# Experts of the mixture stage: which ones share a pass, and in which order the passes run

## The reference

```python
def _hier_moe(h, rg_w, rg_b, re_w, re_b, w_gate, w_up, w_down):
    pg = jax.nn.softmax((ht @ rg_w + rg_b).astype(f32), axis=-1)
    g_val, g_idx = lax.top_k(pg, 1)                      # one of 4 groups
    le = (jnp.einsum('td,ode->toe', ht, re_w) + re_b).astype(f32)
    le = jnp.take_along_axis(le, g_idx[:, :, None], axis=1)[:, 0]
    pe = jax.nn.softmax(le, axis=-1)
    e_val, e_idx = lax.top_k(pe, TOPK_EXPERT)            # 2 of its 8 experts
    ...
    for o in range(N_GROUPS):
        hid = jax.nn.silu(einsum(ht, w_gate[o])) * einsum(ht, w_up[o])
        out = out + jnp.einsum('tef,efd->td', hid * c_o[:, :, None], w_down[o])
```

| group | experts | tokens |
|---|---|---|
| 0 | 0 to 7 | 72 101 67 73 27 38 39 99 |
| 1 | 8 to 15 | 83 98 70 46 47 50 69 97 |
| 2 | 16 to 23 | 110 55 30 40 37 52 94 44 |
| 3 | 24 to 31 | 94 59 51 48 72 42 89 55 |

## Time and profile before

### The profile page before, as it was taken

How to read it: one execution, slowest core, us unless ns; L and a number is a source line. 1 busy time by engine, 2 the same in 40 slices (tenths; PEclk the granted TensorE clock), 3 DMA queues, 4 the chain that set the end, 5 groups by cost and what they waited for, 6 DMA issues and landing times. The chain is left out here.

```text
span 1122.4 us, 13494 instructions
## 1 busy us (share of the span) xinstructions
PE 1015.0 (90%) x5111; PEld 597.1 (53%) x5111; DVE 495.0 (44%) x1214; ACT 274.6 (24%) x629; POOL 161.3 (14%) x150
## 2 busy tenths in 40 slices
PE   6999999975599989999999999996999999979980
PEld 4434777764455456666667455563554444434430
DVE  3477560068815466665665124274721211212214
ACT  3200110130112377566655011120101110101113
POOL 3000000025301131201010000011212122111210
PEclk9999999986899999999999999987999999989995
DMA  9200020032400091000000243455889999999728
GB/s 257 90 19 25 1 76 0 1 43 75 96 1 1 1 256 52 2 1 2 1 2 2 75 150 125 193 218 226 270 305 361 378 390 390 378 367 363 271 49 306
DMA packets 53632, 163.16 MB, mean 145 GB/s; under 512 B 24759, under 2 KB 26871, under 8 KB 41207
## 3 DMA queue, kind: packets, MB, share of 16 engines
q1 hardware_dynamic: 45184, 144.38, 35.8%
q0 software_dynamic: 8384, 17.91, 6.5%
HBM read 145.28 MB, written 26.29 MB: 153 GB/s over the span
## 5 line engine op out<-in xcount | busy, mean ns | idle before, releaser
L1885 PE MATMUL banks<-shared,wout 128*128 128x512 f32 (+1 forms) x416 | 159.4, 612 | 11.3 <-issue 9.6
L1539 PE MATMUL banks<-wout,shared 128*128 128x512 f32 x256 | 112.7, 594 | 0.5 <-PEq L1202 0.5
L364 PE MATMUL banks<-x,wout 128*128 128x512 f32 x256 | 112.0, 594 | 1.1 <-DVE x L405 1.1
L1885 PEld LDWEIGHTS banks<-shared,wout 128*128 128x128 f32 (+1 forms) x416 | 62.6, 175 | 87.9 <-issue 87.7
L1250 ACT ACTIVATE shared<-shared,low 128x640 f32<-128x640 f32 (+7 forms) x128 | 92.9, 729 | 2.6 <-DVE low L1337 2.1
L1933 DVE SCALAR_TENSOR_TENSOR mix_bt<-mix_bt,slot_coef,banks 128x256 f32<-128x256 f32 x26 | 12.5, 480 | 174.0 <-ACT mix_bt L1913 173.9
L1300 PE MATMUL banks<-consts,shared 128*128 128x128 f32 x528 | 77.8, 282 | 4.4 <-ACT shared L1250 3.6
L1907 PE MATMUL banks<-shared,hidt 128*128 128x512 f32 (+1 forms) x208 | 79.6, 595 | 0.8 <-ACT hidt L1917 0.8
L364 PEld LDWEIGHTS banks<-x,wout 128*128 128x128 f32 x256 | 47.8, 190 | 60.2 <-issue 58.1
L1300 PEld LDWEIGHTS banks<-consts,shared 128*128 128x128 f32 x528 | 56.0, 140 | 43.8 <-issue 38.2
L1866 POOL DMA_INDIRECT x_rows<-wout,tok x26 | 41.4, 1593 | 255.2 <-DVE wout L1940 236.5
(11 more groups left out here) (349 smaller groups left out, 1289.6 us busy)
## 6 DMA issues: line engine op xcount, KB each, us to landing
shared<-in_exp_w_down SPq DMA_DIRECT2D x26, 1024.0 KB, 21.1
shared<-in_exp_w_gate SPq DMA_DIRECT2D x26, 1024.0 KB, 10.7
shared<-in_exp_w_up SPq DMA_DIRECT2D x26, 1024.0 KB, 21.3
x<-in_exp_w_gate SPq DMA_DIRECT2D x6, 1024.0 KB, 13.6
x<-in_exp_w_up SPq DMA_DIRECT2D x6, 1024.0 KB, 23.4
x<-in_exp_w_down SPq DMA_DIRECT2D x6, 1024.0 KB, 22.2
shared<-in_x SPq DMA_DIRECT2D x8, 512.0 KB, 7.6
wout<-in_w_in SPq DMA_DIRECT2D x2, 2048.0 KB, 8.5
```

Of the source, the lines that this page charges most:

```text
L364: ins = nc.tensor.matmul(bank[:], slot[:, c, c0:c0 + P], ht[:, c, half * 512:half * 512 + 512], **flags)
L1539: ins = nc.tensor.matmul(psum[n % 4], src[:, i * P:i * P + P], m["wout"][:, k, half * 512:half * 512 + 512], start=k == 0, stop=k == KD - 1)
L1885: ins = nc.tensor.matmul(psum[2 + p][rows].rearrange("p (a f) -> p a f", a=2), xt[:, p, k, rows], wgu[b][:, :, k], start=k == 0, stop=k == ...
```

## The change

The experts are numbered anew: position n of the kernel's tables stands for expert `EXPERT[n]`. The first half holds groups 0 and 2 (experts 0 to 7 and 16 to 23), the second groups 1 and 3. The fixed experts are then 0, 1, 2 and 8, 9, 10 in place of 0, 1, 2 and 16, 17, 18. `FULL` is 5 in place of 7: ten ranked singles and eight pairs, 24 passes in all. The order of the ranked passes is PSPSPPSPSPPSPSSSSS in place of PSSPSSPSSPSSPSSPSSSS. `pick` is written by position, in two instructions for each of the two choices, since the order of the groups is not that of the positions. The number that goes to the weight loads is looked up in `expert`, and that of the extra passes is summed up from the steps between neighbours (`next`). By the table above the paired experts have 27 to 52 tokens in the first half and 42 to 59 in the second.

```diff
--- before.py
+++ after.py
@@ -38,7 +38,8 @@
 NG, EPG, E, DE = 4, 8, 32, 256
 UN, WBUFS = 4, 5
 FIXED = (0, 1, 2, 16, 17, 18)
-RANKED, FULL = E // 2 - 3, 7
+RANKED, FULL = E // 2 - 3, 5
+EXPERT = [2 * EPG * (n % (2 * EPG) // EPG) + EPG * (n // (2 * EPG)) + n % EPG for n in range(E)]
 COLS = len(FIXED) + 2 * FULL + RANKED - FULL
 SLOT_TILES_EXTRA = 21
 OVER_IDS = 24
@@ -92,6 +93,8 @@
         "first8": np.broadcast_to(EPG - np.arange(EPG), (P, EPG)),
         "over": np.broadcast_to(P * np.arange(1, 9), (P, 8)),
         "token": 1.0 * (q[:, None] + P * np.arange(NT)[None, :]),
+        "expert": np.broadcast_to(np.array(EXPERT, np.float32), (P, E)),
+        "next": np.broadcast_to(np.diff(EXPERT, append=E - 1), (P, E)),
         "tie": np.broadcast_to(E - 1.0 - np.arange(E), (P, E)),
         "first": np.broadcast_to(np.repeat([len(FIXED), len(FIXED) + 1], RANKED), (P, 2 * RANKED)),
         "back": np.broadcast_to(np.repeat([FULL, FULL - 1], RANKED), (P, 2 * RANKED)),
@@ -1495,19 +1498,19 @@
             if i == 0:
                 sp.wait_ge(m["o_ready"], NT)
             if i < 4:
-                load_down(nc, d, m, sp, loads[i][0][1], buffer_of(i))
+                load_down(nc, d, m, sp, EXPERT[loads[i][0][1]], buffer_of(i))
             elif i < 6:
-                load_gate_up(nc, d, m, sp, loads[i - 4][0][1], buffer_of(i - 4))
+                load_gate_up(nc, d, m, sp, EXPERT[loads[i - 4][0][1]], buffer_of(i - 4))
             elif i == 6:
                 sp.wait_ge(t_out, 8)
                 sp.wait_ge(m["x_stored"][0], 16 * 4)
-                load_gate_up(nc, d, m, sp, loads[4][0][1], buffer_of(4))
+                load_gate_up(nc, d, m, sp, EXPERT[loads[4][0][1]], buffer_of(4))
         sp.wait_ge(o_done, 2 * NT)
         for j in (2, 3):
-            load_gate_up(nc, d, m, sp, loads[j][0][1], buffer_of(j))
+            load_gate_up(nc, d, m, sp, EXPERT[loads[j][0][1]], buffer_of(j))
         sp.wait_ge(t_out, 12)
         sp.wait_ge(m["x_stored"][1], 16 * 2)
-        load_down(nc, d, m, sp, loads[4][0][1], buffer_of(4))
+        load_down(nc, d, m, sp, EXPERT[loads[4][0][1]], buffer_of(4))
 
     def on_scalar(act):
         def powers(t0, t1, n):
@@ -1660,8 +1663,10 @@
             chain(V.scalar_tensor_tensor(le, oh[:, 0], MASKED, le, ALU.mult, ALU.add))
             top(oh[:, 1], le, lt, EPG, l2, ms)
             for k in range(2):
-                chain.note(V.tensor_tensor(pick[:, k, at].rearrange("p i (g e) -> p i g e", g=NG), bc(gsel, EPG, 3),
-                                           bc(oh[:, k], NG, 2), ALU.mult))
+                for h in range(2):
+                    chain.note(V.tensor_tensor(pick[:, k, at].rearrange("p i (h b e) -> p i h b e", h=2, b=2)[:, :, h],
+                                               bc(gsel.rearrange("p i (b h) -> p i h b", b=2)[:, :, h], EPG, 3),
+                                               bc(oh[:, k], 2, 2), ALU.mult))
             chain.sync()
             tt(sel[:, at], pick[:, 0, at], pick[:, 1, at], ALU.add)
             for i in range(t0, t1):
@@ -1762,7 +1767,7 @@
     statics = [statics[k] for k in (0, 3, 1, 4, 2, 5)]
     singles = [(len(FIXED) + 2 * r + h, [("ranked", h, r)], {h}) for r in range(FULL) for h in range(2)]
     pairs = [(len(FIXED) + FULL + r, [("ranked", h, r) for h in range(2)], {0, 1}) for r in range(FULL, RANKED)]
-    order = statics + [(singles if kind == "S" else pairs).pop(0) for kind in "PSSPSSPSSPSSPSSPSSSS"]
+    order = statics + [(singles if kind == "S" else pairs).pop(0) for kind in "PSPSPPSPSPPSPSSSSS"]
     assert not singles and not pairs and len(order) == COLS
     passes, loads = [], []
     for col, experts, halves in order:
@@ -1965,7 +1970,7 @@
                 if j == len(FIXED):
                     sp.wait_ge(ids_ready, 1)
                 if what[0] == "fixed":
-                    e = what[1]
+                    e = EXPERT[what[1]]
                 else:
                     at = what[1] * RANKED + what[2]
                     e = sp.value_load(m["ids"][0:1, at:at + 1], min_val=0, max_val=E - 1)
@@ -2145,7 +2150,7 @@
                 reduce(rank[:], wins[:], ALU.add)
                 yield
                 tt(wins[:], bc(rank[:], RANKED, 2), bc(bc(m["row"][:, 0:RANKED], 2, 1), RANKED, 3), ALU.is_equal)
-                tt(wins[:], wins[:], bc(m["row"][:, 0:E].rearrange("p (h x) -> p h x", h=2)[:, :, ranked], RANKED, 2), ALU.mult)
+                tt(wins[:], wins[:], bc(by_half(m["expert"]), RANKED, 2), ALU.mult)
                 yield
                 reduce(place[:], wins[:], ALU.add)
                 chain(V.tensor_copy(m["ids"], place[:].rearrange("p h r -> p (h r)")))
@@ -2206,6 +2211,7 @@
                 row_hots("row")
                 yield
                 tt(ovt[:], bc(ovend[:], OVER_IDS, 1), bc(m["row"][:, 0:OVER_IDS], E, 2), ALU.is_le)
+                tt(ovt[:], ovt[:], bc(m["next"], OVER_IDS, 1), ALU.mult)
                 reduce(ovid[:], ovt[:], ALU.add)
                 ts(ovid[:], ovid[:], float(E - 1), ALU.min)
                 chain(V.tensor_copy(ovid[:, OVER_IDS - 1:], ovend[:, E - 1:E]))
```

## The result

The changed kernel takes 1119.37 us (median of 8, 1116.98 to 1123.95) against 1126.58 for the one before (median of 8). The ratio is 0.9935, 95% interval 0.9914 to 0.9957: 7.2 us faster, where no change was forecast. The profiled execution took 1119.59, 4.7 under the profiled one of before; that one lies 2.3 under its own median, so the two traces show only 4.7 of the 7.2.

The account below looks back on a forecast made before the run. Expert stage bound by a full DMA stream, TensorE also full: -2.7 (stream) + 0.4 (`pick`) + 0.6 (after last pair) + 1.4 (clock) + 0.3 (scatter) = 0.0 against 1124.31; median 1.35 above, so 1125.7 us. Range 1119.5 to 1130.5.

Parts of the forecast that it names:

- What bounds the stage: Expert stage, 846 to 1018 us: DMA share 1.00 and TensorE busy 164.69 of 172.20 us, so both are full.
- The removed 21.4 us come back as waits: TensorE's work falls 21.4 us, but waits for weights at L1885 grow from 9.6 to 20 to 28 us.
- The stream, -2.7: Weight loads up to load 26: 174 fewer rows moved by then, so it lands 2.7 us earlier.
- Rival 1: Stream a little quicker, last pair doesn't wait and pays no clock price: -4.4, 1121.3 us; chance 0.24.
- After the last pair TensorE leads: From the last pair to the last gate-up, TensorE sets the time: 57.9 us in place of 57.3.
- The clock: Slow clock after the wait at the last pair costs gate-up 1.4 us, bounds 0 and 2.77.
- The rule of the Trainium skill: Products shorter than the DMA waits between them restart on the slow clock; last pair would pay 1.4 us more.
- Small parts: Last `pick` product on the chain +0.37 us (bounds 0.2 and 0.6); last scatter, 69 rows for 52, +0.3 us.
- Extra passes: A paired expert with over 64 tokens brings an unhidden pass of over 31 us: 1157 us; chance 0.02.

Follow-up runs that it names:

- the turned and the spread kernel before: Kernel before with second-half ranked singles filling slots from 64 on: 1120.48 us; with positions within each half of 64 slots also spread: 1111.71 us.
- the turned pair: Second-half ranked singles filling slots from 64 on, in the kernel before (1120.48 us) and in the changed kernel (1117.04 us).
- early_pairs: Kernel before, 26 passes and old sets, with the pairs close together early (order PSPSPSPSPSPSSSSSSSSS): 1126.21 us, ratio 1.0006.
- regroup_only: Changed kernel with seven full ranks and the old order again, keeping only the new sets: 1124.13 us, ratio 0.9982 to before.
- turned_late: Changed kernel with second-half ranked singles filling slots from 64 on and the last pair moved to loads 27 and 28: 1113.67 us.
- spread_after: Changed kernel with second-half ranked singles filling from slot 64 and positions spread within each half of 64 slots: 1112.34 us, ratio 0.987 to before.

## Why the prediction was wrong

*What bounds the stage: right as far as it goes.* The stream does, with a share of 1.01, and the landing of load 26 starts the last pair. But what binds in the stream is its last engine and not the mean (below).

*The removed 21.4 us come back as waits: right in kind.* TensorE's busy time fell by 13.8 (13 forecast). The waits are 17.8 us, below the 20 to 28 forecast, which fits a stream that was quicker. Without rows the two passes are worth 21.0. Pass 13 could start when forecast (934.58 for 934.7), but not after a wait of 9: pass 11 had already waited 3.46, which the working did not have, and pass 13 then waited 3.43. (By the earlier trace rows TensorE's own pace gives 924.8 for pass 13, not the 925.5 written there, which changes nothing in the sum.) The longest wait was at pass 16, where load 23 let the pair start at 982.00 and not at 986.3: the stream drew ahead of the forecast between loads 18 and 23.

*The stream, -2.7: the step that failed. It was -7.5.* "A row costs 21.5% of 172.2 us over 2,358 = 15.7 ns of all engines" spreads each row over 16 engines. Its count was right: 2,162 rows forecast, 8.87 MB or 2,165 rows moved between 846.3 and 1011 us:

```profile
q1 hardware_dynamic: 7506, 54.18, 80.0%
q0 software_dynamic: 3456, 8.87, 20.5%
```

Against the earlier trace rows the rows' packets took 33.76 us of all engines (20.5% of 164.7) in place of 37.02, 3.3 less and near the forecast. The weights' packets up to the landing took 131.8 (80.0%) in place of 135.2, 3.4 less, where the working had them equal; the last 0.8 is the fuller share. That fits engines that had run less far ahead of the last one. A landing waits for the busiest engine, and by the table this one lost 7.0 us of rows, not 2.7. A pair fills slots from 0 and from 64, a single from 0 only; eight pairs in place of six, with the smaller expert in the low half, took rows off the low slots. I read a share of 1.00 as a wall of bandwidth, but it is a mean over engines of which the last was up to 29 us behind the first. That the place of rows moves the landings is shown by the turned and the spread kernel before. That it made the change's 7.5 rests on the table and on the turned pair, where 2.3 are left of them. Rival 1 (1121.3) comes nearest. The stream did run 2% quicker (383 GB/s for 375), but the rival named no cause, and its last pair does not wait, where the real one waited 3.59 us and paid 1.7 for the clock: that its time came close is luck.

*After the last pair TensorE leads: right*, 59.6 with the clock's 1.7 (57.9 and 1.4 forecast). Moving the last pair later gave 4.6 us by the medians, and 3.4 on top of the turned and of the spread slots each, which fits; one by one these lie within the noise. The early pairs did not settle it.

*The clock: right in size*, 1.7 at the last pair for 1.4. The waits of 3.43 to 5.11 us cost 1.5 to 3.0 each, all but the last hidden. One of 2.19 cost 1.8 (granted clock 0.59 from 964 to 967 us), where before one of 2.10 had cost nothing. Nor did 2.37 (`early_pairs`), 2.61 (`regroup_only`), 2.75 (`turned_late`) and 2.96 (`spread_after`): length alone does not tell. The rule of the Trainium skill that the prediction sets against itself (TensorE: Matmul & The Clock Gate, HAM oscillation) is one for products shorter than the waits between them. Here 13 to 27 us of products lie between two waits, so it was not this case, and the last pair paid 1.7 and not the full 2.77.

*Small parts.* `pick` took 0.51 for four (0.37 for two), so +0.14 for +0.37, my low bound 0.2 being too high. The last scatter took 6.04 with 69 rows, no more than 6.02 with 52: +0.3 was wrong. *Extra passes:* none ran; priced at 31 or more, they take 33 each.

Open: the trace does not say which engine a packet went through. The mapping is the Trainium skill's (the section named above), taken over to gathers and scatters. What supports it is the table: four landings differ from before's as the busiest engine does, within 0.8 us. Of the two that were forecast by it, one came within 1.1 (1006.5 for 1005.4), and one missed by 5.9 (1009.3 for 1003.4). Why executions of one kernel differ by up to 10 us is open too, and with it the 2.5 us by which the medians are further apart than the two traces.

## What to carry to other kernels

A DMA share of 1.00 is a mean over 16 engines, and a transfer lands with its slowest. Where partly filled tiles are gathered or scattered beside a stream, compare the first and the last signal of a transfer before taking the stream for a wall, and try where the rows stand: spreading them over the partitions gave 14.6 us here, twice the 7.2 of the change, without removing a pass. And where two loads feed one pass and TensorE leads from the last such pass on, try that pass later; here it gave 3 to 5 us by the medians.

## What was new of the hardware

Where rows stand in a gathered or scattered tile moves the landings of other queues' transfers: with the same rows and passes, load 26 landed at 1018.5, 1011.5 and 1006.5 us. Down weights' first and last engine finished up to 29 us apart with rows, at most 4 without. Slots that point outside cost next to nothing: GpSimd's queue in the kernel before without rows, 846.3 to 1018.5 us (packets, MB, share of 16 engines; 9.66 MB and 21.5% with rows; 0.40 of the 0.42 MB are 97 rows of the fixed passes):

```profile
q0 software_dynamic: 4318, 0.42, 2.6%
```

A row of 4 KiB took 159 ns of one engine in a gather and 327 in a scatter that adds. The granted clock fell after a wait of 2.19 us, but not after others of 2.10, 2.37, 2.61, 2.75 and 2.96.
